# A column sum issued behind a third weight unit, and two merges that start with two units side by side

## The reference, cut to what matters

```python
def reference(...):
    x = first_block(...)      # MLP, attention mixer, MLP, then rms norm
    return second_block(x, ...)

# end of the first block
h = h + FFN_HALF * _swiglu(_rmsnorm(h, norm_ffn2[i]), ffn2_gate[i], ffn2_up[i], ffn2_down[i])
return _rmsnorm(h, norm_final)

# second block: two layers
for l in range(DEPTH_2):
    h = rms_norm(x, norm_w[l])
    x = x + hybrid_mixer(h, ...)
return rms_norm(x, final_norm_w)

# end of hybrid_mixer: o is the gated delta rule's output, u the convolution branch's
y_a = o.reshape(bsz, seq, DN_V).astype(h.dtype) @ w_dn_out
y_b = (u * jax.nn.silu(z_b)) @ w_cf_out
gate = jax.nn.sigmoid(gate_lg + gate_b).reshape(bsz, seq, N_BRANCH, D_MODEL)
y = gate[:, :, 0] * y_a + gate[:, :, 1] * y_b
return y @ w_out
```

## Time and profile before

| what | value |
|---|---|
| median of 3 runs | 2185.73 us (2185.45 to 2186.78) |
| profiled execution, its own time | 2181.29 us |
| its span, first to last instruction | 2180.0 us |
| mean granted TensorE clock | 0.985 |
| PE busy | 2076.5 us, 95% of the span |
| DVE busy | 1257.8 us, 58% |
| POOL busy | 888.4 us, 41% |
| ACT busy | 883.5 us, 41% |

### The profile page before, as it was taken

One profiled execution on the slowest core, in us unless ns is written; L12 is line 12 of the kernel. 1 busy time (PEld: TensorE's weight loads), 2 busy tenths in 40 slices (PEclk: granted clock), 3 DMA queues, 4 the chain that ended last, 5 costly groups with the idle time before them and its releaser, 6 DMA issues.

```text
span 2180.0 us, 26667 instructions
## 1 busy us (share of the span) xinstructions
PE 2076.5 (95%) x10724; PEld 1656.2 (76%) x10724; DVE 1257.8 (58%) x1944; ACT 883.5 (41%) x1413; POOL 888.4 (41%) x431
## 2 busy tenths in 40 slices
PE   8999999998999999999999999799999999899997
PEld 7888888675666788888887787678778787778775
DVE  5422223757677533222225979898653779898643
ACT  4222233323444543222235385344533475343632
POOL 4444443332113344444444553343334464343342
PEclk9999999999999999999999999999999999999998
DMA  4333333221001232333333222101222322011222
GB/s 154 110 135 97 97 97 106 96 70 39 30 30 49 75 96 91 97 97 97 97 98 94 68 78 69 38 30 29 79 87 87 95 80 69 28 30 40 78 87 78
DMA packets 46186, 169.09 MB, mean 78 GB/s; under 512 B 5232, under 2 KB 6000, under 8 KB 45808
## 3 DMA queue, kind: packets, MB, share of 16 engines
q1 hardware_dynamic: 45344, 165.60, 24.4%
q10 hardware_dynamic: 720, 1.79, 0.2%
HBM read 165.27 MB, written 2.10 MB: 77 GB/s over the span
## 4 chain that ended last, share of the span: by engine, by line
PE 78%; DVE 15%; ACT 6%; issue 1%; POOL 0%; DMA 0%; DVEq 0%; ACTq 0%
PE ps L384 22%; PE ps L386 21%; PE ps L385 21%; PE ps L440 2%; DVE blk_t L1927 1%; DVE outer L1925 1%; DVE cu L1825 1%; PE ps L633 1%; PE ps L617 1%; PE ps L602 1%; ACT dl L1424 1%; ACT whi L987 1%; PE ps L937 1%; DVE dl L2034 1%; PE ps L948 1%
## 5 line engine op out<-in xcount | busy, mean ns | idle before, releaser
L2154 POOL TENSOR_TENSOR wlo<-raw,whi 128x1024 fp32r<-128x1024 f32 x300 | 734.4, 2454 | 904.5 <-ACT whi L987 904.0
L384 PE MATMUL ps<-xh,whi 128*128 128x512 f32 x1584 | 645.4, 407 | 15.1 <-ACT gates L1162 6.2
L386 PE MATMUL ps<-xh,wlo 128*128 128x512 f32 x1584 | 620.4, 392 | 0.0
L385 PE MATMUL ps<-xl,whi 128*128 128x512 f32 x1584 | 619.9, 391 | 0.0
L384 PEld LDWEIGHTS ps<-xh,whi 128*128 128x128 f32 x1584 | 299.3, 189 | 102.1 <-issue 33.4
L987 ACT CAST whi<-raw 128x1024 fp32r<-128x1024 f32 x300 | 312.5, 1044 | 156.2 <-DMA raw<-in_stream 156.0
L385 PEld LDWEIGHTS ps<-xl,whi 128*128 128x128 f32 x1584 | 299.5, 189 | 63.0 <-issue 6.3
L386 PEld LDWEIGHTS ps<-xh,wlo 128*128 128x128 f32 x1584 | 298.9, 189 | 63.9
L1825 DVE SCALAR_TENSOR_TENSOR cu<-up,lcols,cu 128x512 f32<-128x512 f32 x180 | 182.0, 1063 | 0.1
L2190 POOL TENSOR_TENSOR cu<-cu,prod 128x512 f32<-128x512 f32 x60 | 87.6, 1459 | 149.0 <-ACT prod L1229 147.8
L1531 DVE TENSOR_TENSOR ml<-mid,mh 128x512 fp32r<-128x512 f32 x42 | 56.2, 1343 | 152.8 <-ACT mh L1048 152.8
(11 more groups left out here) (354 smaller groups left out, 3048.0 us busy)
## 6 DMA issues: line engine op xcount, KB each, us to landing
raw<-in_stream SPq DMA_DIRECT2D x300, 512.0 KB, 3.6
w1k<-in_w SPq DMA_DIRECT2D x1, 2048.0 KB, 8.1
w1v<-in_w SPq DMA_DIRECT2D x1, 2048.0 KB, 8.0
outT<-h SPq DMA_DIRECT2D x4, 512.0 KB, 2.7
h<-in_xT ACTq DMA_DIRECT2D x2, 512.0 KB, 7.2
h<-in_xT SPq DMA_DIRECT2D x2, 512.0 KB, 7.6
mats<-in_mats ACTq DMA_DIRECT2D x1, 448.0 KB, 10.4
msk<-in_masks SPq DMA_DIRECT2D x1, 258.0 KB, 3.8
```

The costliest lines, as they stand in the source:

```text
L384: pe.matmul(out, wh, hi, start=first, stop=False)
L385: pe.matmul(out, wh, lo, start=False, stop=False)
L386: return pe.matmul(out, wl, hi, start=False, stop=last)
L2154: pool.tensor_tensor(m.wlo[:, slot, :], m.raw[:, slot, :], m.whi[:, slot, :].bitcast(F32), ALU.subtract).then_inc(s.wlo)
```

## The change

Three edits. The order of two names in the list of semaphores changes, and nothing else hangs on it. The second column sum leaves `norm` and becomes `second_norm`, which `layer(0)` calls behind unit 2. And in the two layers' merges, units 0 and 1 are issued side by side: the delta rule's half of both (12 matmuls each), then the convolution's half of both; the wait ahead of them is for the `wlo` of both units.

```diff
@@ norm @@
         sum_rows(ps[:, 6, :], [m.rt[:, 3, :]]).then_inc(s.sums)
-        if e == 3:
-            pe.wait_ge(s.total, TOTALS[4])
-            pe.wait_ge(s.even_squares, 3)
-            sum_rows(ps[:, 7, :], halves(m)[0:2]).then_inc(s.sums)
+
+    def second_norm():
+        pe.wait_ge(s.total, TOTALS[4])
+        pe.wait_ge(s.even_squares, 3)
+        sum_rows(ps[:, 7, :], halves(m)[0:2]).then_inc(s.sums)
@@ merge @@
-        for c in range(KD):
+        if not mixer:
+
+            pe.wait_ge(s.wlo, u0 + 2)
+            for r in range(2):
+                for c in range(2):
+                    for k in range(4):
+                        if c == 0:
+                            pe.wait_ge(s.mix_lo, 8 * g + 4 * r + k + 1)
+                        ins = multiply(u0 + c, 4 * r + k, ps[:, 2 * c + r, :], fh[:, 4 * r + k, :], fl[:, 4 * r + k, :],
+                                       k == 0, k == 3)
+                    if r == 1:
+                        ins.then_inc(s.unit)
+        for c in range(0 if mixer else 2, KD):
             bank = 2 * (c % 2)
@@ layer @@
             x_unit(u0 + 2 * c, ps[:, 2 * (c % 2), :], m.fh, m.fl)
+            if l == 0 and c == 1:
+                second_norm()
             x_unit(u0 + 2 * c + 1, ps[:, 2 * (c % 2) + 1, :], m.fh, m.fl)
```

More of the change, by code:

```diff
@@ L170 @@
     "xr rot vxr vturn blk z1 in_w1v in_mix cmp1 hidden kc2 cmp2 kc_raw kc_rot kcc vc_raw gate_row cmask expd "
-    "score probs pt0 pt1 ptc turned o_new pv cw cturn vcc gts cscore ysum mix_lo h_new yl up wab_lo ab qconv "
+    "score probs pt0 pt1 ptc turned o_new pv cw cturn vcc gts cscore mix_lo ysum h_new yl up wab_lo ab qconv "
     "ab_raw ab_t sq_qkv ab_read decay sums_qkv gl l2 cum d_kk kk_read picked d_pre d_min filled o_sq o_sums "
```

## The result

The changed kernel takes 2188.41 us (median of 20 runs, 2183.00 to 2190.86) where the kernel before takes 2185.12 us on the same chips (20 runs, 2179.27 to 2187.32). The ratio is 1.0017 with an interval of 1.0009 to 1.0025: +3.7 us, between +2.0 and +5.5. The forecast was 2191.0 us in a range of 2187.5 to 2193.5, and +5.3 us. The side forecast as likeliest, slower by more than 0.2%, is missed: the ratio says 0.17% slower, with an interval of 0.09% to 0.25% that holds both 0.2% and the forecast's 0.24%.

The account below looks back on a forecast made before the run. The prediction took PE, busy for 95% of the span, to bound the kernel. Layer 0's entry (+8.6 us) and the two merges (-3.3) summed to +5.3 on 2185.73, giving 2191.0 us, range 2187.5 to 2193.5.

Parts of the forecast that it names:

- The side: Whole kernel: slower by over 0.2%, chance 0.71; within 0.2%, 0.25; faster, 0.04.
- The entry: Layer 0's entry: second sum behind unit 2 reaches DVE 8.75 us later, making PE 8.6 us late at unit 7.
- The rival that the move is harmless: Layer 0's entry: POOL's early `wlo` lets unit 2 fill PE's idle time; only merges count, -3.3 us; chance 0.06.
- The clock: Unit 2 at layer 0's entry: half clock for 4.8 us after PE's restart, losing 2.25 us, included in +8.6.
- The merges: Both layers' merges: 3.3 us of waits vanish, 1.65 us of `wlo` wait comes in; -3.3 us for two layers.
- second case: Whole kernel: same mechanisms, but 1 to 3 us of the delay taken back; +1.5 to +4.3 us, chance 0.20.
- first case: Whole kernel: DVE's chain late at layer 0's entry, merges win a little; +4.4 to +6.3 us, chance 0.58.

Follow-up runs that it names:

- the fillers: Changed kernel plus eight matmuls that nothing reads, behind the first sum, keeping PE busy until unit 2; ratio 1.0014 (1.0004 to 1.0025).
- the last experiment: Changed kernel with POOL's low part of unit 2 moved between the even squares and the small weights; ratio 1.0015 (1.0005 to 1.0026).

## Why the prediction held, point by point

**The entry.** Every step showed in its row: one idle stretch of 6.86 us (predicted 6.9) ended by `wlo`; DVE idle for 8.46 us (about 8); the sum at 1206.26 in a trace that runs 0.73 us early (1207 to 1208); a stall of 6.06 us ahead of unit 4 (about 6); unit 7 8.10 us and `wabh` 8.26 us late (8.6). Moving the sum alone gave +8.35, moving it one unit further +5.23 more. The rival that the move is harmless fell with it: unit 2 could not fill the idle time, since POOL's low part let it open 2.56 us behind the reciprocal's start, as before (2.57).

**The clock.** This term was mis-sized. I took a slow stretch of 4.8 us, the mean of three restarts, and 2.25 us of loss. The stretch was 3.6 us, and the fillers measured a loss of 1.64 (3.6 us at 0.47 each would be 1.7, so the price per slow microsecond was right and the length was not). Unit 2 up to the sum was forecast with 7.70 us and took 7.26; this 0.44 is the gap at DVE (8.75 forecast, 8.34 found), and 0.34 of it is left at `wabh` (8.6 and 8.26). The page TensorE: Matmul & The Clock Gate of the Trainium skill (Part 1) says not to fit the ramp to a count, as it is under 1% of a typical span. Without the term the sum would have been +3.0. The traces agree with the share, 1.64 us of 2185, but not that it can be left out where 0.2% decides. The page also says that the ramp varies from run to run, and the lengths vary here too: 3.6 us here, 4.4 in the last experiment, 3.9, 4.4 and 6.1 in the earlier trace rows. Three restarts were too few to fix a mean.

**The merges.** 1.61 and 1.53 us against 1.65 each. The merge of layer 0 opened 1.65 us later behind the layer's last sum than before, as forecast (16.01 us against 14.36; the row shows 1.49 us of it as a wait), no wait for `fl` was left, and DVE was done with unit 0's tiles at 1607.32 where unit 2 started at 1607.76: 0.44 us of room, forecast 0.35. Alone they gave -3.5 us.

**The side, and the size.** The places gave +5.1 us, the forecast was +5.3, but the ratio came out at +3.7. By the time alone this is the prediction's second case (+1.5 to +4.3, chance 0.20) and not its first (+4.4 to +6.3, chance 0.58). Of what the second case names, the clock did rise earlier, but that is worth the 0.44 us above. PE did not keep the full clock through units 4 to 7: unit 4 ran its first 3.3 us at granted 0.50. So the rows speak for the first case, and the time can't decide, as its interval, +2.0 to +5.5, takes in both.

Where did 1.4 us go? Part of it may be in how the medians come about. The runs of both kernels fall in two groups, and the medians of all runs weigh these by chance. The lower group of the changed kernel (8 runs, 2183.00 to 2185.66) has its median at 2185.06, that of before (6 runs, 2179.27 to 2181.80) at 2180.46; the upper ones (12 and 14 runs) have 2190.14 and 2185.52. Group against group it is **+4.6 us** both times. This split was made after the result was seen, and the lower group of before moves by 0.9 us between sets of runs (2181.4 in the 29 runs beside the first experiments), so it supports +5.1 but does not prove it.

That 2188.41 lies in the range is owed in part to a range wide enough, down to 2187.5, for the second case. Of the 2.6 us between the forecast of 2191.0 and it, 0.6 come from the base: three runs of before, all of the upper group, with 2185.73, where 20 runs have 2185.12. The other 2.0 lie between +5.3 and the +3.3 by which the two medians differ. What part of this is chance stays open; in the profiled pair, places that the change does not touch make 1.7 us.

## What to carry to other kernels

Before a piece of work is moved behind another, ask what the other waits for: a wait of PE for one engine is no free slot if the unit that should fill it waits for a second engine. Then follow who reads the moved result; here a sum of 2 us moved behind a unit of 5.45 held DVE, ACT and POOL for 8.3. And when several units are put side by side, give each its own wait: one wait for the last of them gave back 1.1 of the 2.7 us per merge that the order can win.

## What the runs showed of the hardware

**Two groups of times, 5 us apart, in one kernel on one core.** The runs of the changed kernel with a mean granted clock of 0.986 to 0.987 all take 2183.0 to 2185.7 us; those with 0.982 to 0.983 take 2188.2 to 2190.9, and none lies between. The traces of the ten kernels, which have the same work up to layer 0, show one place where they differ most. In the first block's attention, where PE does short matmuls between waits, the granted clock is 1.00 in three of them and 0.66 to 0.83 in the other seven (windows of 20 us; the third number from the end is the clock, here a mean of stretches at 1.00 and at 0.50). First the kernel before and the changed one, both of the lower group:

```profile
500.00:520.00 20.00, 14.39 (x96) 9.99 (x94) 13.99 (x32) 7.79 (x21) 3.53 (x2) 1.00 0.18 52
```

```profile
500.00:520.00 20.00, 14.16 (x94) 9.66 (x92) 14.37 (x34) 8.20 (x21) 3.58 (x2) 1.00 0.15 52
```

and the kernel with the sum moved alone, of the upper group:

```profile
500.00:520.00 20.00, 16.97 (x74) 12.42 (x73) 10.13 (x27) 5.04 (x12) 0.20 (x1) 0.66 0.08 26
```

PE is busier for less work: 74 matmuls in 16.97 us against 96 in 14.39. The first reciprocal of layer 0 then starts at 1200.6 us or later in every trace with the lower clock there, and at 1196.4 to 1197.8 in the three with 1.00. Measured by DVE's starts, 2.1 to 3.2 us of this arise in the attention stage; further half-clock stretches, near 584 and 737 us, add 1.2 to 1.6 in some traces. The one trace of the changed kernel is of its lower group, so that its own upper group has the same cause is likely but not shown. The change's own place is 680 us further on, so the groups say nothing of it, but a median moves with their mixture.

**DVE's additions beside POOL.** A pair of additions that takes 1.49 us alone took 3.74 us beside POOL's low part and 3.24 us beside its even squares. One low part of 2.40 us moved into their way made the first sum 3.9 us later. POOL is slowed too: the same low part took 2.34 us in the changed kernel and 2.79 where it began beside a DVE addition.
